# Reordering a hybrid decoder step: one block of scores per unit, gated prompt columns first, norm sums a unit later, load waits behind due loads

## The chip, the cores and the metric

The kernel runs on one core of a Trainium2 chip. Its time is the device time of one execution in microseconds (us); the median of several runs is compared. A profiled execution gives the trace. TensorE multiplies matrices, VectorE (DVE) and ScalarE (ACT) work on tiles, GpSimd (POOL) subtracts and clears here, and SyncE (SP) issues nearly all the transfers.

## What is computed

Two layers, each on 512 prompt positions and 8 samples of one position, width 1024. One projection of the normalised residual feeds three branches, whose outputs are gated, added, projected and added to the residual:

```python
h = rmsnorm(x, norm_g)
u_a, z_a, u_b, z_b, q, z_x, g_a, g_b, g_x = split(h @ w_in)
y_a, s_new = s5_branch(u_a, s0, ...)             # complex diagonal scan, 32 groups
y_a = gelu(y_a); y_a = y_a * sigmoid(y_a @ w_glu + b_glu)
o_a = (y_a * silu(z_a)) @ w_br_ssm
v_b = u_b[..., :E] * sigmoid(u_b[..., E:])
c_b = silu(layernorm(causal_depthwise_conv(v_b, width=31)))
o_b = (c_b * silu(z_b)) @ w_br_conv
o_x = attention(q, memory_k, memory_v)           # 4 heads, 256 memory tokens
o_x = (o_x * silu(z_x)) @ w_br_xatt
m = sigmoid(g_a) * o_a + sigmoid(g_b) * o_b + sigmoid(g_x) * o_x
x = x + m @ w_out
```

The outputs are the normalised x of both groups, the new scan states, the convolution buffers and the memory keys and values.

## The kernel before, in words

Every engine has a program of its own, written out by hand in the order in which it shall work, and semaphores tie them. Nothing is planned at build time: an instruction waits only for what stands ahead of it on its engine and for the semaphores that it names.

**Units.** The large products are cut into 72 units a layer, each 128 output columns over all 520 positions (two halves of 260). Weights come through a ring of two slots: SyncE loads a unit's 512 KB into `w_st` (`ring_load`, L307), ScalarE rounds it into `w_hi` (`high`, L1068), GpSimd subtracts to get `w_lo` (L555), and TensorE makes w_hi x h_hi, w_lo x h_hi and w_hi x h_lo (`products`, L635): 48 matmuls for a unit. The slot is free for the next load after the subtraction. ScalarE rounds unit n + 2 when unit n is finished, ahead of keeping unit n's result, in `keep`, `silu`, `gate`, `gate_half`, `value_half`. Units alternate between two accumulators. A `branch` unit has half as many rows: its two halves share one load.

**Order within a layer.** Memory keys and values (L676); units v, q, u (scan input), vb (convolution values and their gates), zx, gx (gates and branch of attention), zb, gb (convolution branch), za, ga (scan branch), out. Between them stand the small products in `mp`, four banks of PSUM:

- attention: `scores(i)` for four blocks of 128 prompt positions (L764), `scores_max(i)` on VectorE (L1542), `exps(i)` on ScalarE (L1146), `probabilities(i)` on VectorE, `turn_probabilities(i)` on TensorE (L600), `keep_probabilities(i)` on ScalarE (L1153), then the product with the values (L797). Scores of a block lie in banks 0 and 1 or 2 and 3 by parity. Then the samples' attention, `spread` (L805) and sums over the cached values (L831);
- the convolution, 31 taps for each of four channel tiles, on VectorE (L1363, `convolution(i, first, end)`), cut into pieces between which other VectorE work stands; `sample_windows` (L1583) and `sample_convolution` for the samples;
- LayerNorm of the convolution: column sums (L929), centring (L1794), squares, sums (L936), variance, square root (L1274), scaling, SiLU (L1278), gating and splitting (L1675, L1676, release L1809);
- the scan, in two halves f: `turn_inputs`, `state_inputs` (L855), `take_inputs`, `scan_up`, `scan_down`, `keep_states` (sets x_done), `lag_matrices` (L865), `keep_lags`, `outputs` (L881, L888), `gelu_outputs`, then through DRAM into `u` (L494 to L498) and the GLU product (L981).

**Merging.** `merge(name, p)` on VectorE takes two branch results out of the accumulators (release L1691) and adds them into xT. TensorE's next unit in the same accumulator waits for it.

**SyncE** issues loads in one written order, and a wait in it holds all that is behind. In `toeplitz(l, half)` it waits for `keep_lags` (L401 is the store of kt), then for that store, and then loads Mt back (eight transfers, L408).

## Time and profile before

| | |
|---|---|
| median of 3 runs | 1299.31 us (1298.57 to 1300.80) |
| profiled execution, its own time | 1295.11 us |
| its span | 1293.3 us |
| mean granted TensorE clock | 0.942 |
| TensorE matmuls busy | 1163.0 us, 90% |
| VectorE busy | 833.9 us, 64% |
| ScalarE, GpSimd busy | 395.3 and 387.6 us |
| moved by DMA | 137.94 MB, 107 GB/s on average |

A granted clock of 1.00 is 2.4 GHz and 0.50 is 1.2 GHz; between them stands a mean over a stretch. In a row of waits, the engine named first waited for what stands behind the arrow.

### The profile page before, as it was taken

How to read it: one execution, taken by the hardware profiler on the slowest of the kernel's cores; microseconds unless marked ns; L12 is line 12 of the kernel's file. 1: busy time of each engine (PE TensorE's matmuls, PEld its weight loads, DVE VectorE, ACT ScalarE, POOL GpSimd, SP SyncE). 2: the span in 40 equal slices, each digit the busy share in tenths (PEclk: the TensorE clock that was granted, in tenths of full speed). 3: DMA queues.
4: the chain of work that ended last, by engine and by line, in shares of the span. 5: the costliest groups of instructions: out<-in, count | busy, mean ns of one | idle time of the engine just before them, and what ended most of it. 6: DMA issues, size and time to landing. Idle time of an engine off the chain costs nothing.

```text
span 1293.3 us, 19959 instructions
## 1 busy us (share of the span) xinstructions
PE 1163.0 (90%) x8322; PEld 1068.3 (83%) x8322; DVE 833.9 (64%) x1223; ACT 395.3 (31%) x556; POOL 387.6 (30%) x183
## 2 busy tenths in 40 slices
PE   5997999979788987989999979999979798979995
PEld 4497989579788987989977968868969798969995
DVE  1889964888779860457825995757857887233322
ACT  4331433142242423223214234233314241312212
POOL 0144234233231432133321522322343222304340
PEclk8998999999897998989999989999989799989998
DMA  7563235732121255154334623547221214422442
GB/s 202 164 226 99 63 115 158 139 88 65 53 82 33 66 121 132 38 134 158 108 99 133 210 64 99 179 126 111 82 68 54 62 35 119 98 66 87 132 131 66
DMA packets 205808, 137.94 MB, mean 107 GB/s; under 512 B 45842, under 2 KB 186570, under 8 KB 204934
## 3 DMA queue, kind: packets, MB, share of 16 engines
q1 hardware_dynamic: 205574, 135.61, 37.5%
q8 instruction: 66, 1.08, 0.4%
q10 hardware_dynamic: 144, 1.05, 0.2%
q14 instruction: 24, 0.20, 0.0%
HBM read 121.86 MB, written 15.72 MB: 106 GB/s over the span
## 4 chain that ended last, share of the span: by engine, by line
PE 67%; DVE 19%; DMA 4%; ACT 3%; SPq 3%; issue 2%; POOL 1%; DVEq 0%; ACTq 0%
PE acc L635 46%; DVE cacc L1363 9%; PE acc L676 4%; PE acc L981 3%; PE mp L831 2%; PE mp L888 2%; PE mp L600 2%; PE mp L764 1%; DMA w_st<-in_w_in 1%; DVE X L1357 1%; PE mp L690 1%; POOL w_lo L555 1%; DVE t L1357 1%; PE mp L805 1%; PE mp L855 1%
## 5 line engine op out<-in xcount | busy, mean ns | idle before, releaser
L555 POOL TENSOR_TENSOR w_lo<-w_st,w_hi 128x1024 fp32r<-128x1024 f32 x144 | 366.0, 2542 | 852.3 <-ACT w_hi L1068 852.0
L635 PE MATMUL acc<-h_hi,w_hi 128*128 128x260 f32 x1664 | 345.4, 289 | 7.6 <-DVEq L1691 7.6
L1068 ACT CAST w_hi<-w_st 128x1024 fp32r<-128x1024 f32 x144 | 150.9, 1048 | 643.7 <-PE acc L635 602.0
L635 PE MATMUL acc<-h_lo,w_hi 128*128 128x260 f32 x1664 | 337.4, 285 | 0.0
L635 PE MATMUL acc<-h_hi,w_lo 128*128 128x260 f32 x1664 | 337.2, 285 | 0.0
L635 PEld LDWEIGHTS acc<-h_hi,w_hi 128*128 128x128 f32 x1664 | 260.6, 191 | 14.5 <-issue 10.0
L635 PEld LDWEIGHTS acc<-h_hi,w_lo 128*128 128x128 f32 x1664 | 259.1, 190 | 0.0
L635 PEld LDWEIGHTS acc<-h_lo,w_hi 128*128 128x128 f32 x1664 | 258.9, 190 | 0.0
L1363 DVE SCALAR_TENSOR_TENSOR cacc<-vx,cw,cacc 128x512 f32<-128x512 f32 x232 | 220.1, 1019 | 3.0 <-DVE xT L1357 1.5
L635 PE MATMUL acc<-bh,w_hi 128*128 128x260 f32 x384 | 85.7, 307 | 32.4 <-ACTq L1201 13.2
L635 PEld LDWEIGHTS acc<-bh,w_hi 128*128 128x128 f32 x384 | 64.9, 207 | 35.6 <-issue 17.3
L635 PE MATMUL acc<-bh,w_lo 128*128 128x260 f32 x384 | 83.5, 302 | 0.0
L1357 DVE TENSOR_TENSOR sg<-acc,sg 128x520 f32<-128x520 f32 x32 | 22.4, 699 | 89.2 <-PE acc L635 86.6
L635 PEld LDWEIGHTS acc<-bh,w_lo 128*128 128x128 f32 x384 | 65.9, 209 | 0.0
L1357 DVE TENSOR_TENSOR X<-X,t 128x16 f32<-128x16 f32 (+9 forms) x88 | 56.9, 647 | 3.0
L676 PE MATMUL acc<-kvw,memg 128*128 128x512 f32 x128 | 55.4, 592 | 0.0
L635 PE MATMUL acc<-m_hi,w_hi 128*128 128x260 f32 x256 | 52.4, 286 | 2.0 <-issue 1.9
L1357 DVE TENSOR_TENSOR q<-q,sg 128x520 f32<-128x520 f32 x8 | 5.6, 701 | 75.1 <-ACT sg L1312 75.1
L635 PE MATMUL acc<-q_r,w_hi 128*128 128x260 f32 x256 | 53.7, 293 | 0.0
L635 PE MATMUL acc<-m_hi,w_lo 128*128 128x260 f32 x256 | 52.2, 286 | 0.0
L635 PE MATMUL acc<-m_lo,w_hi 128*128 128x260 f32 x256 | 52.1, 286 | 0.0
L676 PEld LDWEIGHTS acc<-kvw,memg 128*128 128x128 f32 x128 | 24.2, 190 | 29.2 <-issue 28.9
(276 smaller groups left out, 1481.4 us busy)
## 6 DMA issues: line engine op xcount, KB each, us to landing
w_st<-in_w_in SPq DMA_DIRECT2D x104, 512.0 KB, 3.9
kb<-in_cache_mem_k SPq DMA_DIRECT2D x16, 512.0 KB, 5.7
kb<-in_cache_mem_v SPq DMA_DIRECT2D x16, 512.0 KB, 4.1
w_st<-in_w_out SPq DMA_DIRECT2D x16, 512.0 KB, 4.1
x_scratch<-xT SPq DMA_DIRECT2D x8, 520.0 KB, 6.8
xT<-x_scratch SPq DMA_DIRECT2D x4, 1040.0 KB, 8.0
kvw<-in_w_k SPq DMA_DIRECT2D x8, 512.0 KB, 6.5
kvw<-in_w_v SPq DMA_DIRECT2D x8, 512.0 KB, 3.6
```

The lines of the kernel that those rows point to most:

```text
L555: pool.tensor_tensor(w_lo[:, n % 2, :], w_st[:, n % 2, :], w_hi[:, n % 2, :].bitcast(F32), ALU.subtract).then_inc(w_staged_free, 1)
L600: return pe.transpose(out, in_, ident[0:n, 0:n])
L635: last = pe.matmul(acc_ps[acc][:, a, 0:HC], w_of(w, slot, k), x_of(x, k, a), start=(k == 0 and p == 0), stop=(k == kts - 1 and p == 2))
L676: last = pe.matmul(acc_ps[half][:, m, :], memg[:, k, m * P:(m + 1) * P], kvw[:, i % 3, kk * E:(kk + 1) * E], start=(k == 0), stop=(k == KT ...
L690: last = pe.matmul(mp[:, a, 0:HC], ones[:, :], sq[:, k, a, :], start=(k == 0), stop=(k == KT - 1))
L764: last = pe.matmul(mp[:, 2 * (i % 2) + hd // 2, (hd % 2) * MEM:(hd % 2 + 1) * MEM], q[:, hd, i // 2, (i % 2) * P:(i % 2 + 1) * P], kT[:, h ...
L831: last = pe.matmul(mp[0:32, 2, :], pm[:, m, b, :], kb[:, b % 4, m, :], start=(b == 0 and m == 0), stop=(b == NB - 1 and m == 1))
L888: last = pe.matmul(mp[:, 2 * e + r // 4, (r % 4) * YC:(r % 4 + 1) * YC], V2[:, r, e, :], X2[:, r, e, :], start=False, stop=(r % 4 == 3))
L981: last = pe.matmul(acc_ps[j][:, a, 0:HC], w_dir[:, g, k * 2 * P + j * P:k * 2 * P + (j + 1) * P], u[:, k, a, :], start=(k == 0), stop=(k = ...
L1068: act.copy(w_hi[:, n % 2, :], w_st[:, n % 2, :]).then_inc(w_hi_done, 1)
L1357: run(dve.tensor_tensor(out, a, b, op), behind)
L1363: run(dve.scalar_tensor_tensor(out=out, in0=a, scalar=s, in1=b, op0=op0, op1=op1), behind)
```

## The change

- Attention: block i's scores lie in banks 2 and 3 for even i and in 0 and 1 for odd i (before, the other way round), and the queries' rows of the samples are turned in bank 0. scores(0) no longer waits for st_ev. scores, transposes and units alternate one block per unit on TensorE, and the pieces on ScalarE and VectorE are ordered to fit; `sample_windows` stands ahead of convolution(1).
- Attention's gating: the prompt columns of q are multiplied by zx and split ahead of the samples' results; all four quarters are released together.
- The second convolution's last piece is cut in layer 0, with merge("gx", 1) between.
- zb1 stands ahead of LayerNorm's first column sums, zb3 ahead of its second; gate("gb", 0) on ScalarE stands behind the SiLUs.
- `outputs(1)` stands one unit earlier; the second half's scan is cut around merge("gb", 2) and merge("gb", 3).
- Preparation of layer 1: memory_scaled, state_parameters and powers one merge later.
- SyncE: `toeplitz` is parted into `keep_lags` (the store) and the rest, with a load between; loads of ga are put among the stores and the rows of the next layer.

The bank arithmetic, which appears as `2 * (i % 2)` before and `2 - 2 * (i % 2)` after in six places, is left out below.

```diff
@@ SyncE
-                wait(sp, l, "k_ev", half + 1)
                 kh = k_dram[half * (G // 2):(half + 1) * (G // 2)]
                 kg = kh.rearrange("g h x -> h g x")
-                sp.dma_start(kh.rearrange("(q e) h x -> (e h) q x", e=2), kt[:, :, :]).then_inc(sm["k_out"], 16)
                 wait(sp, l, "k_out", 16 * (half + 1))
...
+            def keep_lags(l, half):
+
+                wait(sp, l, "k_ev", half + 1)
+                kh = k_dram[half * (G // 2):(half + 1) * (G // 2)]
+                sp.dma_start(kh.rearrange("(q e) h x -> (e h) q x", e=2), kt[:, :, :]).then_inc(sm["k_out"], 16)
...
                 gate_loads(l, "gx", 4, 7)
+                keep_lags(l, 0)
+                gate_loads(l, "gx", 7, 8)
                 toeplitz(l, 0)
-                gate_loads(l, "gx", 7, 12)
+                gate_loads(l, "gx", 8, 12)
...
                 gate_loads(l, "gb", 0, 12)
+                keep_lags(l, 1)
+                in_loads(l, "za", E, 0, 1)
                 toeplitz(l, 1)
                 wait(sp, l, "acc_done", 4)
-                wait(sp, l, "k_out", 32)
...
-                in_loads(l, "za", E, 0, 4)
-                gate_loads(l, "ga", 0, 2)
+                in_loads(l, "za", E, 1, 4)
...
+                gate_loads(l, "ga", 0, 1)
                 wait(sp, l, "y_out", 160)
...
-                gate_loads(l, "ga", 2, 6)
+                gate_loads(l, "ga", 1, 6)
...
                     parameter_rows(l + 1)
+                gate_loads(l, "ga", 6, 7)
+                if l + 1 < LAYERS:
                     sp.wait_ge(sm["mem_out"], 16)
                     sp.dma_start(memn[:, :, :].rearrange("p k m -> p (k m)"), m_dram).then_inc(sm["mg_in"], 16)
+                gate_loads(l, "ga", 7, 8)
+                if l + 1 < LAYERS:
                     state_rows(l + 1)
-                gate_loads(l, "ga", 6, 10)
+                gate_loads(l, "ga", 8, 10)
@@ TensorE
                 scores(0)
+                in_unit(l, "u", 1)
                 wait(pe, l, "qs_done", 1)
+                wait(pe, l, "st_ev", 1)
...
                 last.then_inc(sm["qrow_tr"], 1)
+                in_unit(l, "u", 2)
                 scores(1)
-                in_unit(l, "u", 1)
-                in_unit(l, "u", 2)
                 turn_probabilities(0)
+                in_unit(l, "u", 3)
+                scores(2)
                 turn_probabilities(1)
-                scores(2)
+                in_unit(l, "vb", 0)
                 scores(3)
-                in_unit(l, "u", 3)
-                in_unit(l, "vb", 0)
                 turn_probabilities(2)
+                in_unit(l, "vb", 1)
                 turn_probabilities(3)
-                in_unit(l, "vb", 1)
+                in_unit(l, "vb", 2)
                 wait(pe, l, "pT_ev", 4)
...
-                in_unit(l, "vb", 2)
+                in_unit(l, "vb", 3)
                 wait(pe, l, "pv_ev", 1)
                 spread(0)
-                in_unit(l, "vb", 3)
                 in_unit(l, "zx", 0)
...
                 in_unit(l, "zb", 0)
+                in_unit(l, "zb", 1)
...
-                in_unit(l, "zb", 1)
                 in_unit(l, "zb", 2)
+                in_unit(l, "zb", 3)
...
-                in_unit(l, "zb", 3)
...
                 in_unit(l, "za", 0)
+                outputs(1)
                 in_unit(l, "za", 1)
-                outputs(1)
...
                             parameters(l + 1)
-                        elif p == 2:
+                        elif p == 3:
                             state_parameters(l + 1)
@@ ScalarE
+                exps(0)
+                keep("u", 1, u)
                 wait(act, l, "qrow_tr", 1)
...
-                exps(0)
+                keep("u", 2, u)
                 exps(1)
-                keep("u", 1, u)
-                keep("u", 2, u)
                 keep_probabilities(0)
-                keep_probabilities(1)
-                exps(2)
-                exps(3)
                 keep("u", 3, u)
...
+                exps(2)
+                keep_probabilities(1)
                 gate_half(2)
+                exps(3)
                 keep_probabilities(2)
+                value_half(2)
                 keep_probabilities(3)
-                value_half(2)
+                gate_half(3)
...
-                to_v(3)
+                value_half(3)
...
                 silu("zb", 0, q)
+                silu("zb", 1, q)
...
-                silu("zb", 1, q)
...
-                gate("gb", 0)
...
+                gate("gb", 0)
                 gate("gb", 1)
...
                 silu("za", 0, q)
+                gelu_outputs(1)
                 silu("za", 1, q)
-                gelu_outputs(1)
@@ VectorE
                 convolution(0, 0, TAPS)
-                convolution(1, 0, 6)
+                sample_windows()
+                convolution(1, 0, 5)
...
-                sample_windows()
-                convolution(1, 6, 14)
+                convolution(1, 5, 9)
                 scores_max(0)
+                convolution(1, 9, 13)
+                probabilities(0)
+                convolution(1, 13, 19)
                 scores_max(1)
-                convolution(1, 14, 18)
-                probabilities(0)
+                convolution(1, 19, 22)
                 probabilities(1)
-                convolution(1, 18, 24)
                 scores_max(2)
+                convolution(1, 22, 26)
+                probabilities(2)
                 scores_max(3)
-                convolution(1, 24, TAPS)
-                probabilities(2)
+                convolution(1, 26, TAPS)
                 probabilities(3)
...
+                wait(dve, l, "z_ev", 1)
+                for i in range(ET):
+                    tt(prompt_part(q, i), prompt_part(q, i), prompt_part(zx, i), ALU.mult)
+                prompt_split(0)
+                prompt_split(1)
                 convolution(2, c1, c2)
+                wait(dve, l, "pvs_done", NB)
+                prompt_split(2)
+                prompt_split(3)
                 wait(dve, l, "oxT_tr", 1)
...
-                wait(dve, l, "z_ev", 1)
-                for i in range(ET):
-                    tt(q[:, i, :, :], q[:, i, :, :], zx[:, i, :, :], ALU.mult)
-                    split(q[:, i, :, :], q_r[:, i, :, :], i)
-                    dve.sem_inc(sm["br_x_done"], 1)
+                tt(sample_part(q), sample_part(q), sample_part(zx), ALU.mult)
+                run(dve.tensor_copy(sample_part(bh), sample_part(q)))
+                run(dve.tensor_tensor(sample_part(q_r), sample_part(q), sample_part(bh).bitcast(F32), ALU.subtract))
+                dve.sem_inc(sm["br_x_done"], 4)
...
-                convolution(2, c3, TAPS)
+                mid = min(c3 + 5, TAPS)
+                convolution(2, c3, mid)
                 merge("gx", 1)
+                if mid < TAPS:
+                    convolution(2, mid, TAPS)
...
-                scan_up(1)
+                scan_up(1, 0, 3)
                 merge("gb", 2)
                 keep_lags(1)
-                scan_down(1, 4, -1)
+                scan_up(1, 3, 6)
+                scan_down(1, 4, 1)
                 merge("gb", 3)
+                scan_down(1, 1, -1)
                 keep_states(1)
...
                 merge("ga", 0)
                 if l + 1 < LAYERS:
                     parameters(l + 1)
-                    memory_scaled(l + 1)
                 merge("ga", 1)
                 if l + 1 < LAYERS:
                     angles(l + 1)
-                    state_parameters(l + 1)
                 merge("ga", 2)
                 if l + 1 < LAYERS:
-                    powers(l + 1)
+                    state_parameters(l + 1)
+                    memory_scaled(l + 1)
                 merge("ga", 3)
                 if l + 1 < LAYERS:
+                    powers(l + 1)
                     level_factors(l + 1, 0, 1)
```

## Rows read from the trace of the kernel before

**Rows 1.** The page's part 1: busy us, share of the span, instructions.

```profile
PE 1163.0 (90%) x8322; PEld 1068.3 (83%) x8322; DVE 833.9 (64%) x1223; ACT 395.3 (31%) x556; POOL 387.6 (30%) x183
```

**Rows 2.** TensorE's waits over the whole span: us in total, times, longest.

```profile
PE acc L981 <- DMA u<-y_scratch: 15.9, 2, 8.0
PE mp L929 <- DVEq L1592: 15.8, 2, 7.9
PE mp L764 <- DVEq L1583: 14.7, 2, 7.3
PE acc L635 <- ACTq L1201: 13.2, 3, 5.4
PE acc L635 <- DVEq L1809: 11.0, 8, 3.2
PE acc L635 <- DVEq L1691: 7.6, 2, 7.0
...
PE acc L635 <- DVEq L1682: 6.5, 2, 3.2
PE mp L888 <- ACT X L1284: 6.1, 2, 3.1
```

**Rows 3.** Timeline of TensorE, layer 0, LayerNorm: start, us, what, idle before.

```profile
341.28 5.43 PE L929 MATMUL mp<-cv,ones 128*128 128x260 f32 x16 [7.89 <-DVEq L1592]
...
388.81 0.80 PE L635 MATMUL acc<-bh,w_hi 128*128 128x260 f32 x2 [0.38 <-DVEq L1809]
```

**Rows 4.** Stretches behind gaps: busy us of each engine, then PEclk, DMA share, GB/s.

```profile
406.70:413.60 6.90, 6.90 (x33) 6.90 (x34) 6.56 (x12) 1.09 (x1) 0.00 (x0) 0.50 0.02 5
...
568.00:573.20 5.20, 5.20 (x24) 5.20 (x25) 0.00 (x0) 0.00 (x0) 1.71 (x1) 0.50 0.35 103
```

**Rows 5.** The page's part 5: the weights' cast and subtraction.

```profile
L555 POOL TENSOR_TENSOR w_lo<-w_st,w_hi 128x1024 fp32r<-128x1024 f32 x144 | 366.0, 2542 | 852.3 <-ACT w_hi L1068 852.0
...
L1068 ACT CAST w_hi<-w_st 128x1024 fp32r<-128x1024 f32 x144 | 150.9, 1048 | 643.7 <-PE acc L635 602.0
```

**Rows 6.** Timeline of VectorE in attention, layer 0.

```profile
134.48 2.74 DVE L1363 SCALAR_TENSOR_TENSOR cacc<-vx,cw,cacc 128x512 f32<-128x512 f32 x4
...
140.43 8.07 DVE L1363 SCALAR_TENSOR_TENSOR cacc<-vx,cw,cacc 128x512 f32<-128x512 f32 x6
```

**Rows 7.** Groups of ScalarE from 118 to 170 us: busy us, mean ns.

```profile
L1146 ACT ACTIVATE pr<-mp,stat 128x256 f32<-128x256 f32 x16 | 7.3, 483 | 3.5 <-DVEq L1545 3.5
...
L1153 ACT COPY pT<-mp 128x1024 f32<-128x1024 f32 x4 | 3.9, 1020 | 0.1
...
L1146 ACT ACT_TABLE_LOAD x1 | 1.3, 1283 | 0.0
```

**Rows 8.** The chain that ended last, parts of layer 0: start, us, what.

```profile
130.91 1.97 PE mp L764 x8
132.87 11.53 PE acc L635 x96
...
274.74 14.27 DVE cacc L1363 x15
...
503.92 4.75 DMA y_scratch<-U
508.69 5.12 DMA u<-y_scratch
```

**Rows 9.** Timeline of SyncE's issues around toeplitz(1), layer 0.

```profile
455.42 0.34 SPq L401 DMA_DIRECT2D k_scratch<-kt  x1
...
462.25 17.38 SPq L307 DMA_DIRECT2D w_st<-in_w_in  x4
```

**Rows 10.** Timeline of VectorE, first and last of the 38 instructions of powers.

```profile
597.07 0.07 DVE L1425 MEMSET pw<- 128x16 f32 x1 [0.19 <-DVE m_lo L1697]
...
609.62 0.21 DVE L1373 COPY pw<-tiny 128x64 f32<-128x64 f32 x1
```

More of the change, by code:

```diff
@@ L753, in scores @@
                 def scores(i):
-                    if i < 2:
+                    if i == 0:
                         wait(pe, l, "q_ev", 4)
                         wait(pe, l, "kT_ev", 1)
-                        if i:
-                            wait(pe, l, "qrow_ev", 1)
-                        else:
-                            wait(pe, l, "st_ev", 1)
+                    elif i == 1:
+                        wait(pe, l, "qrow_ev", 1)
                     else:
@@ L763, in scores @@
                     for hd in range(HEADS):
-                        last = pe.matmul(mp[:, 2 * (i % 2) + hd // 2, (hd % 2) * MEM:(hd % 2 + 1) * MEM],
+                        last = pe.matmul(mp[:, 2 - 2 * (i % 2) + hd // 2, (hd % 2) * MEM:(hd % 2 + 1) * MEM],
                                          q[:, hd, i // 2, (i % 2) * P:(i % 2 + 1) * P], kT[:, hd, :], start=True, stop=True)
@@ L772, in turn_probabilities @@
                             j = 2 * hd + m
-                            last = transpose(mp[:, 2 * (i % 2) + j // 4, (j % 4) * P:(j % 4 + 1) * P],
+                            last = transpose(mp[:, 2 - 2 * (i % 2) + j // 4, (j % 4) * P:(j % 4 + 1) * P],
                                              pr[:, i % 2, hd, m * P:(m + 1) * P], P)
@@ L1145, in exps @@
                     for hd in range(HEADS):
-                        last = act.activation(pr[:, i % 2, hd, :], mp[:, 2 * (i % 2) + hd // 2, (hd % 2) * MEM:(hd % 2 + 1) * MEM],
+                        last = act.activation(pr[:, i % 2, hd, :], mp[:, 2 - 2 * (i % 2) + hd // 2, (hd % 2) * MEM:(hd % 2 + 1) * MEM],
                                               ACT.Exp, bias=stat[:, 16 + 4 * i + hd:17 + 4 * i + hd], scale=SCALE,
@@ L1661, in _, with split, prompt_part, sample_part @@
                 dve.sem_inc(sm["pm_ev"], 1)
+                def split(value, low, i):
+                    run(dve.tensor_copy(bh[:, i, :, :], value))
+                    run(dve.tensor_tensor(low, value, bh[:, i, :, :].bitcast(F32), ALU.subtract))
+                def prompt_part(t, i):
+                    return t[:, i, :, 0:4 * C]
+                def sample_part(t):
+                    return t[:, :, :, 4 * C:HC]
                 output_matrices(0)
@@ L1671, in _ @@
                 dve.sem_inc(sm["ox_done"], 1)
-                def split(value, low, i):
-                    run(dve.tensor_copy(bh[:, i, :, :], value))
-                    run(dve.tensor_tensor(low, value, bh[:, i, :, :].bitcast(F32), ALU.subtract))
-                wait(dve, l, "z_ev", 1)
-                for i in range(ET):
-                    tt(q[:, i, :, :], q[:, i, :, :], zx[:, i, :, :], ALU.mult)
-                    split(q[:, i, :, :], q_r[:, i, :, :], i)
-                    dve.sem_inc(sm["br_x_done"], 1)
+                tt(sample_part(q), sample_part(q), sample_part(zx), ALU.mult)
+                run(dve.tensor_copy(sample_part(bh), sample_part(q)))
+                run(dve.tensor_tensor(sample_part(q_r), sample_part(q), sample_part(bh).bitcast(F32), ALU.subtract))
+                dve.sem_inc(sm["br_x_done"], 4)
                 def merge(name, p):
@@ L1726, in level, with scan_up @@
                     tt(dst, dst, tb, ALU.add)
-                def scan_up(f):
-                    for k in range(6):
+                def scan_up(f, first, end):
+                    for k in range(first, end):
                         level(f, k, (2 << k) - 1, C >> (k + 1))
@@ L1794, in _ @@
                     dve.sem_inc(sm["cent_done"], 1)
-                scan_up(0)
+                scan_up(0, 0, 6)
                 wait(dve, l, "lsq_used", 1)
```

11 lines of the change are left out of this document (7 added, 4 removed).

## The prediction

> **What bounds the kernel now.** I read the page's shares first: TensorE is busy for 90% of the span and VectorE for 64% [rows 1]. So the time is TensorE's work plus its gaps, and the question for each edit is which gap it closes and what ends that stretch next. The second view was TensorE's waits [rows 2]: eight rows, 90.8 us, nearly all in pairs, one in each layer. The third was its granted clock behind a gap [rows 4]: 0.50 (1.2 GHz), where 24 matmuls take 5.2 us, 0.217 each, against 0.120 in a stretch without gaps (96 in 11.53) [rows 8]. So a gap costs itself and then about half of the slow stretch behind it, 1.7 to 3.5 us. The sixteen column-sum matmuls show it: 5.43 us behind a gap of 7.89 [rows 3]; the same number behind none would take about 3.5 at the ratio of these two prices.
>
> The last view was VectorE against GpSimd. Four convolution taps take 2.74 us alone, 0.685 each; six take 8.07 where two of GpSimd's w_lo subtractions (2.54 each [rows 5]) fall in [rows 6]. 8.07 - 4.11 leaves 3.96, so each subtraction takes about 2 us from VectorE. The Trainium skill, "SBUF — State Buffer", section "Who interferes with whom", says that a VectorE instruction with two SBUF inputs and a GpSimd one that reads SBUF lock each other out for a whole instruction. By that the price is at most one subtraction, 2.54; by it LayerNorm and the path to x_done, two subtractions each, would lose 1.1 more apiece, 4.3 over both layers. The trace agrees, with 2.0, and 2.0 is what I use.
>
> A unit is 48 matmuls, 5.76 us [rows 8]; one subtraction follows each. I call the time at which work is reached against before its lead.
>
> **The change, part by part** (both layers unless said).
>
> *Scores.* scores(0) no longer waits for sample_windows, so the 7.35 us of its wait go (14.7 for two), with about 1.8 of slow clock behind it and two small waits of 0.8: 10.7 per layer. What is late next: blocks now pass one at a time. After scores(1), VectorE has six taps (4.1 plus up to two thefts, 4.0) before scores_max(1), 1.4 us; then ScalarE's exps(1), four at 0.483 overlapping to 1.9; only then keep_probabilities(0), 0.95 with its wait, releases scores(2). From the end of scores(1) that is the normalisation of block 0 (1.4) + 8.1 + 1.4 + 1.9 + 1.0 = 13.8, less some 4 us by which the taps' start precedes it. TensorE has one set of transposes (0.9) and unit u3 (5.76) for cover. So a wait of about 3 to 4 us stands before scores(2), about 1 before scores(1) (its q row is copied behind exps(0) and a cast), about 0.6 before the fourth transposes. 5.5 plus 1.2 to 1.8 of slow clock remain; the lead is about 4. Bounds: 0 (all thefts fall on these pieces) and 10.7 (none).
>
> Exps and sigmoids alternate now, so two more table loads of 1.28 us [rows 7] per layer stand on ScalarE; the edit of gate("gb", 0) saves one. ScalarE has room: a cast (1.05) and a subtraction (2.54) follow a unit's end, 3.6 in 5.76, so each cast can be 2.1 late for nothing. I put the loads at nothing, bounded by 1.3 per layer. The Trainium skill, "ScalarE: Activation LUTs", section "Table sets: the hidden batching unit", speaks against the edit: calls should be batched by set. By it the sum would lose 2.6 per layer if both loads were on the path.
>
> *Prompt columns first.* The wait for the last quarter of q (6.5 for two) and 1.8 of slow clock behind each. Eight 512-column multiplies and subtractions, about 0.7, and four casts of 0.43 move ahead of the value sums' end: in layer 1 they lie under TensorE's L831 loop, and 3.2 + 1.8 = 5 is won. In layer 0 input_matrices (six operations, 7.4 us) stands ahead of them as well; all four quarters are now released together, and I find VectorE 2 to 4 us behind. I take 0 there.
>
> *The split convolution (layer 0 alone; in layer 1 c3 + 5 is 31, nothing moves).* 15 taps, 14.27 us, end just before the 7.0 gap [rows 2, 8]. With five taps ahead, merge("gx", 1) waits for its matmuls instead and the gap goes. But the ten taps, three sample convolutions (5.0) and conv(3, 0, 8) (5.9 plus a theft) still precede merge("gx", 2), and VectorE idled about 4.7 us before the two halves of merge 1. I find gate("gx", 6) waiting 6 to 8 us. So this gap moves and is not closed, and VectorE decides when the mean starts: of layer 0's 4 us of lead I keep 2. In layer 1 merge 1 already waited for TensorE, the two go in step, and the lead of 4 + 5 = 9 survives. Together 11. Bounds: 2 and 24.
>
> *Norm sums a unit later.* The wait for the convolution is 7.9 per layer [rows 2]. zb1 ahead of it fills 5.76, and of the 1.9 lost to the slow clock behind it I expect 1.75 back, since 2.1 of gap is left: 7.5 per layer, 15. Bounds 11.5 and 19.6. Then LayerNorm: gate("gb", 0) leaves ScalarE's queue ahead of the SiLUs. Before, the last release came at 388.8, 42.1 after the sums' end (346.7) [rows 3]. Now: centring 3.3, scan 13.8, variance and reciprocal 4.2, square root 0.7, four scalings 3.4, then four quarters of 2.05 with two subtractions on them, since their casts follow the SiLUs: 3.3 + 13.8 + 4.2 + 0.7 + 3.4 + 8.2 + 4.0 = 37.6. The gain is 4.5; without the second theft 6.5; I take 5.5 per layer, 11. Late next: branch("gb", 0)'s low weights, ready at about 29.8 after the sums, under the same quarters.
>
> *Load queue.* toeplitz(1) held za's first load behind the lag matrices' way to DRAM and eight Mt loads: SyncE issues kt at 455.42 and the weights at 462.25 [rows 9]. Now kt is followed by za0 at once, some 6.4 earlier; it needs to land by the end of gate("gb", 7), and with 4 to 5 us of landing it does. The third wait of the same row is ga6 behind parameter and state rows, 14 + 11 small loads. All 13.2 us of [rows 2] go, with the half of the slow clock behind three gaps, 7.1: 20.3. Bounds 13.2 and 21. Two 1 MB and 512 KB loads meet at y_in; ga0 lands under za3's matmuls.
>
> *outputs(1) a unit earlier.* The wait for y_in, 15.9 for two, ends a chain of gelu, ten stores, their landing (4.75) and the load of u (5.12) [rows 8], 19.8 from the outputs' end. Moving it by 5.76 would give 5.76 a layer. But scan_down(1, 1, -1) (5.2) now stands behind merge("gb", 3), and four copies of 0.48 after it: counted from the end of branch 7, x_done comes at 1.7 + 5.2 + 2.1 + two thefts 4 = 13, TensorE is there at 5.76 + 3.5 = 9.3. The outputs' second half starts at 11 to 13, and they end at 15 to 20 where they ended at 18.6. TensorE is busy for 18.2 of the 19.8, so 1.6 of gap is left and most of the 2.7 of slow clock is saved. 3 per layer, 6. Bounds -1 and 8.5 each.
>
> *Into layer 1.* powers moves behind merge("ga", 3): from 597.07 to 609.83, 12.8 us, 8.5 without its thefts [rows 10]. That wins the 1.95 gap before output unit 0 and its slow clock. But accumulator 0 is freed by VectorE's first x addition: merge to +5.2, powers 8.5 + 4, level_factors 1.6, addition 0.9, so at 20.3 from branch 7's end, where TensorE wants it at 11.5. 8.8 of gap plus 2 of slow clock, against 3.8 before: I take -7. Bounds -10 and +2.
>
> **The sum** against the profiled execution's 1295.1 (span 1293.3): 11 + 15 + 11 + 20.3 + 6 - 7 = 56.3, so 1238.8. The median of the runs is 1299.31, 4.2 above that execution, so 1243.
>
> **Rivals.**
> 1. *VectorE is the bound in both layers.* Every gap closed ahead of the mean comes back at scores(2) or at a merge: layer 1's 9 become 2, LayerNorm gives 3 a layer, y nothing, the tail -10. The load queue gives 17, between its bounds. 4 + 11.5 + 6 + 17 + 0 - 10 = 28.5: 1271. For it: VectorE had hardly a gap from 82 to 170 in layer 0. Against: in layer 1 it idled 12 us before the third convolution.
> 2. *The thefts fall elsewhere.* No wait at scores(2) (5.5 more in layer 1), outputs at once (5.5 a layer), powers with no theft (5): 56.3 + 5.5 + 11 + 5 = 78, 1221.
> 3. *Slower.* ScalarE works in order, and exps(0) now stands ahead of u1's cast and copy. If scores_max comes late, every cast behind an exps is late, and TensorE stops at the next unit for what exceeds 2.1. Eight exps against 56 us: it decides from about 9 us late for each. The taps between them are three to six, 2 to 8 us with thefts, so it can't reach that by the rows. Worked out at 10 each: 8 x 7.9 = 63 against 56, 1306.
> 4. *Nothing.* The gaps add up again at the next wait, 1299.
>
> **Chances.** Forecast 0.52, rival 1 0.23, rival 2 0.17, rival 3 0.05, rival 4 0.03. From no change, 0.2% (2.6 us) is about what a measurement can tell. So faster 0.92, same 0.03, slower 0.05. The range reaches into rivals 1 and 2: 1218 to 1272.
>
> **What would show it.** TensorE's wait at scores(0) gone and one of 3 to 4 us before scores(2); in layer 0 the 7.0 wait of the accumulator moved to gate 6; L929 waiting 2 us and running near 3.5; no ScalarE wait for weights at za0 and ga6; a wait inside L888 behind branch 7; a new wait near 9 us for the first x additions of layer 0. I am wrong if TensorE waits for w_lo in attention, if outputs(1) ends no earlier than 20 us behind branch 7, or if that wait near the tail is absent.

## The result, and the profile after

The changed kernel took 1281.08 us (median of four runs, 1278.74 to 1282.3) against 1298.94 for the kernel before on the same chip: ratio 0.9858, 95% interval 0.984 to 0.9876, 18 us faster. A later group gave 1283.16 and 0.983 (0.9777 to 0.9882). The forecast was 1243 with 1218 to 1272: the sign was right, and two thirds of the gain were missing. Its profiled execution took 1282.3 us (span 1280.5), 12.8 less than that of before: it is the slowest of its four, and that of before lies 4 under its median, so what is read from the two traces falls 5 us short of the medians. In what follows, one of attention_back's six runs, which took 2684.04 us, is in the median of the table and not in the ratio. The page's busy time of TensorE, to be set beside [rows 1]:

```profile
PE 1171.2 (91%) x8322; PEld 1074.6 (84%) x8322; DVE 833.8 (65%) x1229; ACT 397.9 (31%) x558; POOL 393.3 (31%) x183
```

The same 8322 matmuls were busy for 8.2 us longer. So TensorE waits 21 less (109.3 against 130.3, span less busy) and works 8 longer. I summed its busy time by what the granted clock lacks to 1.00, over windows of 1 us: 50.3 us lost before, 56.7 after. The forecast had counted on some 12 to 18 less (7.1 in the load queue, 3.5 at the norm sums, 1.8 at the prompt columns, up to 5.4 at the outputs). TensorE's waits (us in total, times, longest), beside [rows 2]:

```profile
PE acc L646 <- DVEq L1895: 9.1, 1, 9.1
PE acc L646 <- POOL w_lo L566: 8.3, 3, 3.3
PE mp L898 <- DVEq L1776: 8.0, 2, 4.0
PE mp L940 <- DVEq L1603: 7.4, 2, 3.7
PE mp L773 <- ACT pT L1163: 7.2, 2, 3.6
...
PE acc L646 <- DVEq L1842: 5.9, 6, 2.2
...
PE acc L646 <- DVEq L1721: 5.3, 2, 4.7
PE mp L611 <- DVEq L1571: 5.1, 1, 5.1
...
PE acc L991 <- DMA u<-y_scratch: 4.2, 2, 2.7
PE acc L646 <- DVEq L1712: 4.2, 1, 4.2
```

Most of these waits were forecast: 3.6 before scores(2), the wait for x_done inside the outputs (8.0 for two), 9.1 for the first x addition of layer 0, and the 13.2 behind ScalarE's casts and the 14.7 at scores(0) gone. Two were not: 5.1 at the transposes of v_last, and 3.3 in each layer for w_lo at branch gb 0, which the forecast had hidden under the quarters. What failed is the sum of the stages. Each column is the length of a stretch of TensorE's timeline in us, cut at the same matmuls in both kernels:

| stretch | before | after | difference | forecast |
|---|---|---|---|---|
| start to ktok's transposes, layer 0 (unchanged work) | 76.35 | 77.62 | +1.3 | 0 |
| to sK's transposes (attention) | 137.9 | 137.3 | -0.6 | -4 |
| to the second half of outputs(0) (gx, zb, LayerNorm) | 192.3 | 195.9 | +3.6 | -11 |
| to the GLU product | 107.2 | 106.7 | -0.5 | -8.8 |
| to layer 1 | 144.6 | 143.3 | -1.4 | 0 |
| layer 1, to sK's transposes | 184.1 | 185.9 | +1.9 | -4 |
| to the second half of outputs(0) | 188.1 | 179.8 | -8.4 | -18 |
| to the GLU product | 110.5 | 104.5 | -5.9 | -10.8 |
| to the end | 152.2 | 149.5 | -2.7 | 0 |

Half of what is missing lies in the two stretches with LayerNorm.

### The profile page after: what moved, and what is told of

Its sections match the earlier page's. It is cut to its first block, busy times and chain, and to the rows that moved or that the text cites. A ratio compares the mean times of both kernels' runs of the same rounds, so it can differ in the third digit from the quotient of the medians.

```text
span 1280.5 us, 19964 instructions
## 1 busy us (share of the span) xinstructions
PE 1171.2 (91%) x8322; PEld 1074.6 (84%) x8322; DVE 833.8 (65%) x1229; ACT 397.9 (31%) x558; POOL 393.3 (31%) x183
## 4 chain that ended last, share of the span: by engine, by line
PE 59%; DVE 31%; DMA 3%; issue 2%; ACT 2%; SPq 2%; POOL 1%; DVEq 0%; ACTq 0%
PE acc L646 40%; DVE cacc L1374 10%; PE acc L687 4%; DVE X L1368 3%; DVE t L1368 2%; PE acc L991 2%; PE mp L898 2%; PE mp L611 2%; DVE cv L1368 1%; PE mp L701 1%; PE mp L816 1%; PE mp L865 1%; PE mp L841 1%; PE mp L808 1%; SPq L500 1%
## 5 line engine op out<-in xcount | busy, mean ns | idle before, releaser
L566 POOL TENSOR_TENSOR w_lo<-w_st,w_hi 128x1024 fp32r<-128x1024 f32 x144 | 371.1, 2579 | 833.4 <-ACT w_hi L1078 833.0
L646 PE MATMUL acc<-h_hi,w_hi 128*128 128x260 f32 x1664 | 349.1, 292 | 5.3 <-DVEq L1721 5.3
L646 PEld LDWEIGHTS acc<-h_hi,w_hi 128*128 128x128 f32 x1664 | 263.6, 193 | 14.0 <-issue 8.3
L646 PEld LDWEIGHTS acc<-h_hi,w_lo 128*128 128x128 f32 x1664 | 262.1, 193 | 0.0
L1374 DVE SCALAR_TENSOR_TENSOR cacc<-vx,cw,cacc 128x512 f32<-128x512 f32 x232 | 205.7, 955 | 4.0 <-DVE xT L1368 2.1
L646 PE MATMUL acc<-bh,w_hi 128*128 128x260 f32 x384 | 82.6, 298 | 18.4 <-POOL w_lo L566 8.3
L646 PE MATMUL acc<-bh,w_lo 128*128 128x260 f32 x384 | 80.7, 293 | 0.0
L1368 DVE TENSOR_TENSOR X<-X,t 128x16 f32<-128x16 f32 (+9 forms) x88 | 60.9, 693 | 3.0
L646 PEld LDWEIGHTS acc<-bh,w_lo 128*128 128x128 f32 x384 | 62.9, 200 | 0.0
L646 PEld LDWEIGHTS acc<-m_hi,w_hi 128*128 128x128 f32 x256 | 40.6, 194 | 9.9 <-issue 9.2
```

The source lines that it names most:

```text
L566: pool.tensor_tensor(w_lo[:, n % 2, :], w_st[:, n % 2, :], w_hi[:, n % 2, :].bitcast(F32), ALU.subtract).then_inc(w_staged_free, 1)
L646: last = pe.matmul(acc_ps[acc][:, a, 0:HC], w_of(w, slot, k), x_of(x, k, a), start=(k == 0 and p == 0), stop=(k == kts - 1 and p == 2))
L1368: run(dve.tensor_tensor(out, a, b, op), behind)
L1374: run(dve.scalar_tensor_tensor(out=out, in0=a, scalar=s, in1=b, op0=op0, op1=op1), behind)
```

## The experiments

Eighteen kernels ran, most of them the changed kernel with one part undone. The last column is the ratio less that of the changed kernel (0.9858; in the last two groups 0.983), by 1299 us; each is good to some 4 us, from queue_alone down to 6. taps_moved and combo4 ran in another group than after_again, and by their ratios alone are good to some 9; by the medians they stand 1 and 28 below it.

| kernel | median us | ratio to before (95%) | against the changed kernel |
|---|---|---|---|
| zb1_back | 1285.61 | 0.9912 (0.9892 to 0.9933) | +7.0 |
| spread_full | 1274.95 | 0.9827 (0.9803 to 0.9852) | -4.0 |
| powers_back | 1274.32 | 0.9824 (0.9802 to 0.9846) | -4.4 |
| outputs_back | 1285.02 | 0.9904 (0.9878 to 0.993) | +6.0 |
| queue_back | 1320.64 | 1.0176 (1.015 to 1.0201) | +41.3 |
| split_back | 1279.71 | 0.986 (0.9834 to 0.9885) | +0.3 |
| gb0_back | 1279.53 | 0.9855 (0.9829 to 0.9881) | -0.4 |
| attention_back | 1286.37 | 0.9902 (0.9878 to 0.9926) | +5.7 |
| queue_alone (on the kernel before) | 1283.27 | 0.9864 (0.9827 to 0.9901) | |
| ln_back | 1287.97 | 0.9889 (0.9847 to 0.993) | +4.0 |
| scan_ahead | 1271.96 | 0.9775 (0.9736 to 0.9815) | -10.8 |
| combo1 | 1266.23 | 0.9739 (0.9701 to 0.9777) | -15.5 |
| after_again | 1283.16 | 0.983 (0.9777 to 0.9882) | 0 |
| taps_cut | 1281.15 | 0.9807 (0.9757 to 0.9857) | -3.0 |
| combo2 | 1257.80 | 0.9645 (0.9595 to 0.9696) | -24.0 |
| combo3 | 1255.09 | 0.9609 (0.956 to 0.9657) | -28.7 |
| taps_moved | 1282.28 | 0.9822 (0.977 to 0.9874) | -1.0 |
| combo4 | 1255.07 | 0.9622 (0.957 to 0.9674) | -27.0 |

**LayerNorm: zb1, gate gb 0, and both.**

```diff
 zb1_back (TensorE; ScalarE likewise)
-                in_unit(l, "zb", 1)
                 wait(pe, l, "acc_done", ET)
...
+                in_unit(l, "zb", 1)
 gb0_back (ScalarE): gate("gb", 0) ahead of the four SiLUs again; ln_back: both
```

> The changed kernel with units zb1 and zb3 back behind the two column sums; everything else as changed. The forecast gave zb1's move 7.5 us a layer, 15 in all: by it this kernel takes about 1296 against 1281. Rival, the chain of VectorE: the last convolution tile, the mean, LayerNorm and its release are one chain, and a unit ahead of the mean only moves TensorE's wait from the mean to the release. By it TensorE's wait at the mean grows by 5.8 a layer and the waits at branch gb 0 shrink by as much, and the time is 1281 within 3.

> The changed kernel with gate gb 0 back in ScalarE's queue ahead of LayerNorm's SiLUs. The forecast put its move at 5.5 us a layer, 11 in all: 1292. Rival: LayerNorm's chain from the mean to the release was 4.1 us shorter in the profile of the change, and with the wait of 3.3 for w_lo that the move makes, the move is worth about 2 a layer: 1285.

> The changed kernel with both edits around LayerNorm undone at once: zb1 and zb3 behind the column sums and gate gb 0 ahead of the SiLUs. The forecast gave the pair 26 us: 1307. Chain of VectorE: both edits shorten or cover the same chain from the mean to the last release (48.5 us before in layer 1, 44.4 changed, 45.8 with zb1 back, 43.9 with gb 0 back), so alone each is worth 0 to 5 and together about 4 a layer: 1287 to 1290.

TensorE's waits of zb1_back, of gb0_back and of ln_back:

```profile
PE mp L939 <- DVEq L1603: 15.8, 2, 7.9
PE acc L646 <- DVEq L1842: 9.1, 6, 3.0
...
PE acc L646 <- POOL w_lo L566: 1.7, 1, 1.7
```

```profile
PE acc L646 <- DVEq L1842: 12.5, 8, 3.2
...
PE mp L940 <- DVEq L1603: 7.4, 2, 3.7
...
PE acc L646 <- POOL w_lo L566: 1.7, 1, 1.7
```

```profile
PE mp L939 <- DVEq L1603: 15.8, 2, 7.9
PE acc L646 <- DVEq L1842: 11.0, 8, 3.2
```

The wait at the mean is 7.9 with zb1 behind it and 3.7 with zb1 ahead, to a tenth, in both layers and in every kernel here that keeps the nine taps behind merge gx 3: it runs from the end of branch gx 7, not from VectorE's backlog. Layer 1, from the end of the mean's sums to VectorE's last instruction for the release: 42.0 us before, 42.0 in ln_back, 40.1 in zb1_back, 37.6 in gb0_back, 37.7 in the changed kernel. So the forecast 37.6 was right, but not its cause: the move of gate gb 0, for which the forecast booked the 4.5, is worth nothing here, and it is zb1's and zb3's order that frees ScalarE for the square root (VectorE waits 0.7 for it, before and in zb1_back 3.2; in zb1_back ScalarE is busy until 990.8 with the cast and the SiLU of zb3, which TensorE finishes only behind the sums, and loads the square root's table behind them). With zb1 back, gate gb 0's move takes 1.9 from the same way (42.0 against 40.1). With gate gb 0 behind the SiLUs, w_lo for branch gb 0 comes 3.3 late instead. Taken together the two edits are worth 4 us by ratio and 7 by medians, and with the interval of 6 hardly more than 10, of 26 forecast.

**What sets the mean: taps_cut and taps_moved.**

```diff
 taps_cut: eight taps of the fourth tile left out
-                convolution(3, 8, 22)
+                convolution(3, 8, 14)
 taps_moved
-                convolution(3, 8, 22)
+                convolution(3, 8, 28)
                 merge("gx", 3)
-                convolution(3, 22, TAPS)
+                convolution(3, 28, TAPS)
```

> The changed kernel without eight taps of the fourth channel tile, between merge gx 2 and merge gx 3 (the convolution is incomplete: the kernel leaves work out). Alone they take 8 by 0.685, 5.5 us in each layer. Forecast: TensorE's lead at the mean is its own, the wait for the convolution 3.7 at most, so the kernel gains up to 3.7 a layer, and only if VectorE is not then waiting for merge gx 3. Chain of VectorE: it waited 5.8 and 5.5 us for merge gx 3 behind these taps already, so taps ahead of it are nearly free, nothing moves, and what sets the mean are the nine taps and the sample convolution behind merge gx 3, 8 to 9 us, on which a unit has no hold: 1281 within 2.

VectorE in layer 0, the changed kernel, then taps_cut:

```profile
316.38 9.37 DVE L1374 SCALAR_TENSOR_TENSOR cacc<-vx,cw,cacc 128x512 f32<-128x512 f32 x14 [0.24 <-DVE xT L1368]
331.55 0.70 DVE L1368 TENSOR_TENSOR xT<-acc,sg 128x520 f32<-128x520 f32 x1 [5.80 <-issue]
...
335.32 10.33 DVE L1374 SCALAR_TENSOR_TENSOR cacc<-vx,cw,cacc 128x512 f32<-128x512 f32 x9 [0.25 <-DVE xT L1368]
```

```profile
318.65 4.07 DVE L1374 SCALAR_TENSOR_TENSOR cacc<-vx,cw,cacc 128x512 f32<-128x512 f32 x6 [0.24 <-DVE xT L1368]
334.03 0.70 DVE L1368 TENSOR_TENSOR xT<-acc,sg 128x520 f32<-128x520 f32 x1 [11.31 <-PE acc L646]
```

The eight taps became wait, 11.31 for 5.80, and TensorE's waits stayed what they were, but for one of 1.7 for w_lo in layer 1, which went. VectorE's work ahead of merge gx 3 is not what the mean waits for. That speaks against rival 1 of the forecast too, for this stretch.

> The changed kernel with six of the nine taps that stood behind merge gx 3 put ahead of it, where VectorE waited 5.8 us in layer 0 and 5.5 in layer 1 for TensorE. One chain from the end of branch gx 7: merge gx 3, nine taps, a sample convolution, the mean, LayerNorm, the release. By it the wait at the mean (3.7) goes, the sums run at full clock (1.8 less), and since the release follows the mean by a fixed time, all of it stays: 5.5 a layer, 1270 against 1281. Rival, the forecast's way of reading gaps one by one: the units behind are busy anyway and the release waits of 5.5 a layer come from w_lo as much as from LayerNorm, so that an earlier mean wins at most its own 3.7 in one layer: 1277.

It won nothing. The wait at the mean did vanish, and another took its place at branch gx: GpSimd's next two subtractions in layer 0, the changed kernel, then taps_moved, and TensorE's wait in it:

```profile
323.95 4.06 POOL L566 TENSOR_TENSOR w_lo<-w_st,w_hi 128x1024 fp32r<-128x1024 f32 x1 [16.78 <-ACT w_hi L1078]
329.72 2.39 POOL L566 TENSOR_TENSOR w_lo<-w_st,w_hi 128x1024 fp32r<-128x1024 f32 x1 [1.71 <-ACT w_hi L1078]
```

```profile
323.12 10.45 POOL L566 TENSOR_TENSOR w_lo<-w_st,w_hi 128x1024 fp32r<-128x1024 f32 x2 [16.63 <-ACT w_hi L1078]
...
331.31 0.80 PE L646 MATMUL acc<-bh,w_hi 128*128 128x260 f32 x2 [3.58 <-POOL w_lo L566]
```

Six taps more ran there without a break (20 in 13.34, 0.667 each, no theft from VectorE, by which the forecast meant time that a subtraction takes from it), and the two subtractions took 10.45 where the same two took 6.45. The taps of the changed kernel end at 325.75 and its first subtraction 2.3 later; those of taps_moved, begun at 315.71, end at 329.05, and two subtractions of 2.3 fit from there to 333.57. In layer 1 the wait for w_lo was 5.7. My chain theory gave 1270; it left out that the subtractions stand in it. In taps_cut, where no tap runs over it, the first of the two took 2.38.

**The clock in attention: spread_full and attention_back.**

```diff
 spread_full
-        qrow = zr("qrow", 4608, [NB, E])
+        qrow = zr("qrow", 4608, [P, E])
...
-   ident[0:NB, b:b + 1].to_broadcast([NB, P]), qrow[:, :]
+   ident[:, b:b + 1].to_broadcast([P, P]), qrow[:, :]
...
+                run(dve.memset(qrow[:, :], 0.0))
```

> The changed kernel, but the matmuls that spread the samples' query rows (eight of 8 rows by 512 columns, in two bursts of 3.7 us) contract over all 128 rows, of which 120 are cleared by one VectorE instruction in each layer. The output is the same. Theory of the few rows: those bursts are what makes the clock fall to 0.50 in a stretch with no gap (821 to 827 and 833 to 838 us, 5.1 us lost in layer 1, 3.4 in layer 0); by it the stretch stays at 1.00, and the transposes of sK come 3 to 5 us earlier in each layer. In the total 3 to 8 us of it show, since VectorE's chain takes a part. Rival: the clock falls there from the waits ahead, at scores(2), or from something in the column units; then the same slow stretches stand and the time is 1281 within 2.

The two bursts in layer 1 of the changed kernel, and its windows (busy us, granted clock, DMA share, GB/s):

```profile
817.33 4.22 PE L816 MATMUL mp<-qrow,ident 8*128 8x512 f32 x8
829.97 3.69 PE L816 MATMUL mp<-qrow,ident 8*128 8x512 f32 x8
```

```profile
816.00:819.00 3.00, 3.00 (x16) 1.00 0.00 0
819.00:822.00 3.00, 3.00 (x7) 0.73 0.00 0
822.00:825.00 3.00, 3.00 (x16) 0.50 0.59 178
825.00:828.00 3.00, 3.00 (x19) 0.63 0.60 174
...
831.00:834.00 3.00, 3.00 (x10) 1.00 0.99 319
834.00:837.00 3.00, 3.00 (x16) 0.50 0.52 131
```

spread_full, a window over its second burst (822.99 to 826.78) and one behind it:

```profile
824.00:827.00 3.00, 3.00 (x11) 1.00 0.63 179
827.00:830.00 3.00, 3.00 (x28) 1.00 0.98 320
```

TensorE is busy all the time, and its clock falls to 1.2 GHz in or behind each burst of 8 rows; over 128 rows, with the same columns and the same 3.7 us, it does not. All the traces here agree. Between the first burst and sK's transposes TensorE is never idle, and the clock costs it (length times what the granted clock lacks to 1.00) 1.7 to 5.1 us in the six stretches of the old order, 3.4 to 6.8 in the 24 of the new order with 8 rows, and 0.0 in the ten with 128 rows (two layers of spread_full and of combo1 to combo4). The stretch from ktok's to sK's transposes took 134.0 in layer 0 (137.3 in the changed kernel's first profile, 137.1 in its second) and 134.8 in layer 1 (139.6). The Trainium skill, "TensorE: Matmul & The Clock Gate", section "Part 1: The HAM clock gate", describes a monitor that sets the clock by how busy TensorE has been. If that is the busy time that the profile shows, the trace does not agree for these windows: it is 3.00 of 3.00 in each of them at either clock.

> The changed kernel with attention's scores, transposes, units and VectorE pieces in their old order and banks, sample_windows behind the first six taps, and both bursts of spread at their old places, two units apart. The forecast gave this part 4 us a layer up to the transposes of sK, 8 in all: 1289. Rival, the clock: the new order wins 3 to 4 a layer in waits and loses 3 to 5 a layer in two stretches at 0.50 behind the bursts, which now stand one unit apart: 1281 within 2, with the stretch's idle time up by 2.5 a layer and its slow clock down by 2 to 5.

The waits and units of the new order are worth 5.7 by ratio (5.3 by medians), near the 8 forecast, and the bursts cost clock in both orders, by an amount that differs between executions: with the same instructions the stretch in layer 0 took 135.5 to 140.3 us over the profiles of kernels with the new order and 8 rows, and in the old one 137.9 before, 139.9 in attention_back and 141.4 in queue_alone. TensorE's idle time ahead of the bursts is steadier: 8.9 us in a layer in the old order, 6.2 to 6.6 in the new one with 8 rows.

**outputs(1) and the cut scan.**

```diff
 outputs_back: outputs(1) and gelu_outputs(1) behind za1 again
 scan_ahead
-                scan_down(1, 4, 1)
+                scan_down(1, 4, -1)
                 merge("gb", 3)
-                scan_down(1, 1, -1)
```

> The changed kernel with outputs(1) and its gelu back behind za1. The forecast put this move at 3 us a layer won: by it 1287. Rival, the clock: outputs(1) one unit earlier meets a wait of 4.0 us for x_done and then 12 us at 0.50, 5.8 lost, about as much as the wait for y_in that it shortens from 7.9 to 2.7 with its 4 to 5 us of slow clock. By it the wait of 4 and its slow stretch vanish, the one for y_in is back at 6 to 8, and the time is 1281 within 3.

> The changed kernel with the last two steps of the second half's scan_down back ahead of merge gb 3; outputs(1) stays a unit earlier. The wait of 4.0 us for x_done and the 12 us at 0.50 behind it are to go, 9.8 in each layer; for it merge gb 3 comes about 5 later, and the first unit that needs an accumulator waits for it. The forecast's steps make it even: 5.2 later against 5.2. Theory of the clock: a gap ahead of a 260-column unit costs itself and 2 to 3 us of slow clock, one ahead of the 72-column outputs 5.8, so that the exchange wins 2 to 3 a layer: 1276.

The outputs' second half, layer 0, and windows over it in the changed kernel; then the same matmuls in scan_ahead:

```profile
487.90 7.07 PE L898 MATMUL mp<-X,V 128*128 128x72 f32 x32 [4.03 <-DVEq L1776]
```

```profile
488.00:491.00 3.00, 3.00 (x15) 0.50 0.00 0
491.00:495.00 4.00, 4.00 (x20) 0.50 0.01 4
495.00:499.00 4.00, 4.00 (x20) 0.50 0.31 42
499.00:503.00 4.00, 4.00 (x33) 0.94 0.82 142
```

```profile
484.21 3.74 PE L898 MATMUL mp<-X,V 128*128 128x72 f32 x32
```

A gap of 4.0 was followed by more than 11 us at 0.50: 5.8 lost, beside the gap. The forecast had read 1.7 to 3.5 behind a gap [rows 4, 8], and it priced this one by them. But the first row of [rows 4] stands behind the gap of 3.07 ahead of these same 72-column matmuls in outputs(0), and it ends at 413.60, when the clock was not back. The kernel before, behind that row, and the same place in layer 1:

```profile
413.60:416.00 2.40, 2.40 (x13) 0.50 0.00 0
1030.70:1041.00 10.30, 10.30 (x48) 0.50 0.02 7
```

So 4.9 and 5.1 were lost there already. Read over the traces of ten kernels here, gaps of 3.0 to 4.4 ahead of the 72-column outputs were followed by 4.4 to 5.9 us lost, every time; gaps of 3.2 to 11.6 ahead of products of 256 or 260 columns by at most 3.0, where no second gap came soon after.

In the changed kernel outputs(1) also ended no earlier: 20.5 and 20.4 us behind the end of branch gb 7, where it had been 18.8. The unit that the move gained went into the gap and the slow clock. In scan_ahead, with the scan's last steps ahead of the merge, the 32 matmuls take 3.74; the price was a wait of 1.12 at the accumulator and 1.2 us a layer more for y_in. The gain, 10.8 by ratio and 9.1 by medians, was more than either theory gave. outputs_back, which keeps the cut, lost 6.0 (3.9 by medians). So the move is worth about what was forecast for move and cut together, and the cut made for it took more than that back. No kernel undid both.

**The load queue.**

> The changed kernel with SyncE's whole order as before. The forecast gave that order 20.3 us (13.2 of waits, 7.1 of slow clock): by it this kernel takes about 1301 against 1281. Rival: the load of za0 is late no more often than before, but with the other units moved the waits it leaves are partly filled by the waits for w_lo, VectorE and y_in that follow, and the order is worth 8 to 12: 1289 to 1293. Second rival: with outputs(1) a unit earlier its loads of Mt meet a queue that is behind, and the order is worth more than 20.

> The kernel before with the changed order of SyncE alone. The forecast gave that order 20.3 us: 1299 becomes 1279, with the three waits of TensorE behind ScalarE's late casts (3.4, 4.4, 5.4) gone. Rival: only these waits and the slow clock behind two of them go, and the wait for y_in (7.9 a layer) grows by a part of it, since the path from VectorE's scan to y_in is not shorter: 8 to 13 us, 1286 to 1291.

queue_alone is the kernel before with SyncE's order alone changed (the second half of the diff in the section on the change). It takes 17.7 us by ratio (12.9 to 22.5), 20.3 forecast, and so as much as the whole change. Without that order the other edits lose 23 us against before, and 41 against the changed kernel. SyncE in queue_back, then in the changed kernel, layer 0:

```profile
484.20 27.70 SPq L307 DMA_DIRECT2D w_st<-in_w_in  x3
511.94 8.32 SPq L494 DMA_DIRECT2D y_scratch<-U  x8
```

```profile
466.66 12.18 SPq L307 DMA_DIRECT2D w_st<-in_w_in  x3
496.35 7.03 SPq L500 DMA_DIRECT2D y_scratch<-U  x8
```

The gelu ends at 501.97 in queue_back, and its first store is issued ten us later, behind a load of ga that waits for its slot; here the stores are issued as soon as the gelu ends (496.33). TensorE's wait for y_in in queue_back:

```profile
PE acc L980 <- DMA u<-y_scratch: 22.4, 2, 11.6
```

It is 4.2 in the changed kernel. TensorE also waits 12.3 behind ScalarE's late casts, where the changed kernel has no such wait, and 8 more of its busy time are lost to the clock. Together these are most of the 41. That outputs(1) a unit earlier can be used only if no load stands ahead of its stores is argued from this; no kernel put back the queue and the outputs together. Of the rivals that I wrote, 8 to 12 was wrong, and "more than 20" right without saying how much more.

**powers, and the cut of the second convolution.** powers_back puts memory_scaled, state_parameters and powers one merge earlier on VectorE, and TensorE's part with them; split_back sets `mid = TAPS`.

> The changed kernel with memory_scaled, state_parameters and powers of layer 1 back at their places one merge earlier. The forecast put their move at 7 us lost: by it this takes 1274, the wait of 9.06 us for the first x addition is gone and the 1.95 ahead of output unit 0 is back. Rival: the time comes back ahead of merge ga 3 (powers stands then before it), and the kernel takes 1281 within 2.

> The changed kernel with the last piece of the second convolution tile whole again ahead of merge gx 1; this touches layer 0 alone. By the forecast VectorE sets the end of that stretch either way and the wait of 7 us at unit gate 6 moves back to where it was: 1281 within 2. Rival: with the cut TensorE waits for VectorE twice (5.1 at the transposes of v_last, 4.7 at gate 6) and VectorE then for TensorE (5.8 at merge gx 3), and each such pair costs: without the cut the stretch from sK's transposes to the mean in layer 0 is 2 to 5 us shorter and so is the kernel, 1276 to 1279.

The wait of TensorE for the first x addition, 9.06, went, and the 1.95 ahead of output unit 0 came back, with 1.40 behind it. The kernel won 4.4 by ratio and 6.8 by medians, as forecast for the step. split_back changed nothing: TensorE waits 7.0 once where it waited 5.1 and 4.7.

**Combinations.** combo1 is spread_full with powers_back; combo2 adds scan_ahead; combo3 adds this, and combo4 the taps of taps_moved:

```diff
 combo3 (ScalarE), behind LayerNorm's square root
+                wait(act, l, "acc_ready0", use["gb"] + 1)
+                high(l * UNITS + unit["gb"] + 2)
                 for i in range(ET):
                     wait(act, l, "ln_done", i + 1)
...
 (gate("gb", 0), behind the SiLUs, no longer rounds these weights)
```

> The changed kernel with the bursts of spread over all 128 rows and powers, state_parameters and memory_scaled back one merge earlier. If the two are independent the gains of 5 and 6 add: 1269 to 1270. If the lead of the first is taken again in layer 1 by the wait at the mean, about 1273.

> The bursts of spread over 128 rows, powers and its neighbours back one merge earlier, and the scan's last two steps back ahead of merge gb 3. If all three are independent 1266 less 9 is 1257. If the lead is taken by the wait for y_in, 1262.

> The same three, and the rounding of branch gb 0's weights ahead of LayerNorm's SiLUs while gate gb 0's sigmoid stays behind them. The wait of 3.3 us for w_lo goes in each layer. If LayerNorm's chain of VectorE sets the end, the later quarters wait instead and the subtraction now falls on VectorE's scalings: within 2 us of the kernel with three edits. If w_lo did, 3 to 6 less.

> The kernel with four edits (128-row bursts of spread, powers back, scan ahead, weights of branch gb 0 rounded ahead of the SiLUs) and the six taps ahead of merge gx 3. By the chain 1255 less 8 to 11 is 1244 to 1247; if only the mean's own wait counts, 1251.

> The changed kernel once more, beside the others of this group: 1281 within 2 by every theory, and from the transposes of ktok to those of sK 135 to 140 us in layer 0, wherever the slow stretches behind the bursts of spread fall in this execution.

The gains add: 4.0, 4.4 and 10.8 make 19.2, and combo2 won 24.0 with an interval of about 6 (by medians 22.0 and 25.4). combo3's 2.7 more by medians lie within what can be told; its wait for w_lo gave way to one of 3.7 behind ScalarE. combo4 added nothing, as taps_moved had not. The two fastest, combo3 at 1255.09 and combo4 at 1255.07, can't be told apart; combo3 is 28 us below the changed kernel of its group (1283.16) and 47 below the kernel before (1301.67).

## Why the prediction was wrong

**The step that failed: "Norm sums a unit later", 7.5 + 5.5 a layer, 26 in all.** It booked the 5.8 us that zb1 fills ahead of the mean, and beside it LayerNorm's shorter way from the sums to the release. But one chain on VectorE, with the sums in it, runs from the end of branch gx 7 to the release: in layer 1 62.1 us before (950.2 to 1012.3) and 59.6 changed (949.4 to 1009.0). The units between only cover it. zb1 ahead of the sums no longer stands behind them, where TensorE then waits for w_lo and the release; the sum counted its cover at the one place and did not take it away at the other. What the chain lost is 2.5: 4.3 behind the sums, less 1.8 ahead of them, where a third subtraction of GpSimd stretched VectorE's last instruction from 0.23 to 1.75. ln_back: 4 us by ratio and 7 by medians, in both layers together. That is some 20 of the 38 missing.

**outputs(1), 6.** The move gave 4 to 6. The cut of the scan cost 9 to 11 by scan_ahead. The forecast had x_done right, 13 us behind branch gb 7, but let the outputs end at 15 to 20: its price for the slow clock, up to 3.5, came from a row that ended before the slow stretch did, and 5.8 were lost. If the two add, about 10 to 12 are missing.

**Scores, 8.** The waits came as forecast (6.2 of idle time left in layer 1, 5.5 forecast). The order is worth 5.7; the bursts of 8 rows, which the forecast never mentioned, cost 4 to 6 over both layers, and they now stand one unit apart. In the first profile of the change they took the whole of the gain. About 2 to 8 missing.

**Prompt columns, 5 in layer 1 and 0 in layer 0.** Right in layer 1: from sK's transposes to turn_inputs(0) 46.6 became 41.6. In layer 0 the wait grew from 3.2 to 4.2 and the stretch by 2.0. No kernel undid this part alone.

**The split convolution.** The gap moved and was not closed, as forecast; of the waits, 5.1 at v_last's transposes was not named, and neither was VectorE's 5.8 for merge gx 3. split_back: no loss and no gain.

**Load queue, 20.3.** Right in size (17.7) and in place. Not seen: that the earlier outputs depend on it.

**powers, -7.** Right: -4.4 by ratio, -6.8 by medians, 9.06 of wait for 8.8 forecast.

**The rivals.** Rival 1 gave 1271 and came nearest, not for its reason: taps_cut shows VectorE waiting for TensorE where it was to be the bound, and it too had left 11.5 to zb1. Rival 2 went the wrong way: x_done and powers waited as forecast. Of rival 3 nothing was seen.

**The signs.** Of the three signs of being wrong one came: outputs(1) ended 20.4 to 20.5 us behind branch gb 7, and 20 was the mark. Of the signs of being right two came short: the column sums waited 3.7 for 2 and ran 5.3 to 6.7 for 3.5, and gate gx 6 waited 4.7 where 6 to 8 were expected. The others came.

These account for most of the missing 38 us. They are not independent, as the load queue shows, and each is uncertain by 3 to 6 us; how the rest is shared out stays open.

## What to carry to other kernels

When a chain on one engine runs from a fixed point to a release, moving covered work from one of its waits to another is worth nothing; add up the chain and the cover once, over the whole stretch, and never a gain for each wait. Price a gap by what runs behind it, 4.4 to 5.9 us ahead of 72-column matmuls and at most 3 ahead of wide ones here, and follow the slow clock to its end before you read its price. Look for low clocks in stretches without a gap, too. Before a result is produced earlier, see that no blocked load stands ahead of its stores.

## What the runs showed of the hardware

- The granted clock fell to 0.50 (1.2 GHz) with TensorE busy for 3.00 of 3.00 us, behind bursts of eight matmuls of 8 rows by 512 columns; the same over 128 rows, 120 of them zeros, kept 1.00, in each of the ten stretches that have them.
- Behind gaps of about the same length the slow clock lasted longer ahead of narrow matmuls: 4.4 to 5.9 us lost ahead of 72 columns, at most 3.0 ahead of 256 or 260. Why is not shown.
- GpSimd's subtraction and VectorE's taps hold each other up in either direction: nine taps took 10.33 us with two subtractions in them (2.83 and 2.50), and two subtractions took 10.45 under 20 unbroken taps of 0.667. The first of these two began at 323.12 and seems to have done nothing until the taps ended at 329.05. The Trainium skill, "SBUF — State Buffer", section "Who interferes with whom", gives the shared port to whoever issues first, for one whole instruction. By that one tap, 0.667, would be the most that a subtraction waits; the trace disagrees, with some nine taps, as far as the spans of GpSimd, which the profile gives roughly, can tell. Why VectorE keeps the port there and loses it in the nine taps behind merge gx 3 stays open.
